# Two wider pitches in SBUF for the split operands of a three-layer fp32 kernel

## The reference, cut to what matters

```python
def peer_ffn(x, norm_ffn, w_query, sub_keys, expert_down, expert_up):
    xn = rmsnorm(x, norm_ffn)
    ...
        q = (xi @ w_query).reshape(B, PEER_CHUNK, PEER_HEADS, 2, PEER_HALF)
        s = jnp.einsum('bthpd,hpnd->bthpn', q, sub_keys)
        ... # top 16 of each half, top 16 of the pairs, idx, gates g
        u = jnp.take(expert_down, idx, axis=0)
        act = jax.nn.gelu(jnp.einsum('btd,bthkd->bthk', xi, u).astype(jnp.float32))
        v_sel = jnp.take(expert_up, idx, axis=0)
        return jnp.einsum('bthk,bthkd->btd', (g * act).astype(xi.dtype), v_sel)

x = x + hgrn_gmlp_mixer(x, ...);  x = x + peer_ffn(x, ...)   # layer 0
x = x + mla_moba_mixer(x, ...);   x = x + peer_ffn(x, ...)   # layer 1
x = x + merged(pool branch, dilated attention) @ w_out       # second block
return _rmsnorm(x, final_gain)
```

## Time and profile before

| | |
|---|---|
| median of 3 runs | 2086.08 us (2085.38 to 2088.28) |
| span of the profiled execution | 2086.7 us |
| PE busy | 2064.9 us (99%), 11,872 products |
| PE weight loads busy | 1768.4 us (85%) |
| DVE, ACT, POOL busy | 1462.7, 1290.6, 373.7 us |
| DMA | 376 MB, 180 GB/s |
| granted TensorE clock | 0.999 of full speed |

### The profile page before, as it was taken

How to read it: one execution, slowest core, us unless ns; L and a number is a source line. 1 busy time by engine, 2 the same in 40 slices (tenths; PEclk the granted TensorE clock), 3 DMA queues, 4 the chain that set the end, 5 groups by cost and what they waited for, 6 DMA issues and landing times.

```text
span 2086.7 us, 31212 instructions
## 1 busy us (share of the span) xinstructions
PE 2064.9 (99%) x11872; PEld 1768.4 (85%) x11872; DVE 1462.7 (70%) x2611; ACT 1290.6 (62%) x2205; POOL 373.7 (18%) x183
## 2 busy tenths in 40 slices
PE   8999999999999999999999999999999999999998
PEld 7788988888888888887888888888888888888888
DVE  7969988889855555567589888889655555543456
ACT  6665688877654444466656788777544444554674
POOL 1447700000000000012378000000000000045241
PEclk9999999999999999999999999999999999999999
DMA  6445755555565665664357555555566666676444
GB/s 228 152 162 170 227 180 166 169 172 166 172 194 190 196 193 191 195 214 141 122 171 222 182 164 171 163 172 171 187 195 192 192 194 191 205 221 195 129 153 140
DMA packets 108459, 376.25 MB, mean 180 GB/s; under 512 B 12373, under 2 KB 17909, under 8 KB 107413
## 3 DMA queue, kind: packets, MB, share of 16 engines
q1 hardware_dynamic: 107444, 369.00, 55.9%
q0 software_dynamic: 864, 5.24, 1.2%
HBM read 367.87 MB, written 1.08 MB: 177 GB/s over the span
## 4 chain that ended last, share of the span: by engine, by line
PE 91%; DVE 7%; ACT 1%; issue 0%; DMA 0%; POOL 0%; SPq 0%; DVEq 0%; ACTq 0%
PE ps L184 27%; PE ps L178 14%; PE ps L179 14%; PE ps L180 14%; PE ps L185 13%; PE ps L1086 3%; PE ps L1109 1%; PE ps L1065 1%; DVE WL L166 1%; DVE arena L1340 1%; DVE arena L791 1%; DVE arena L788 0%; DVE arena L1401 0%; DVE arena L1406 0%; DVE arena L1409 0%; DVE arena L1337 0%
## 5 line engine op out<-in xcount | busy, mean ns | idle before, releaser
L161 ACT ACTIVATE WH<-raw 128x1024 fp32r<-128x1024 f32 x680 | 717.2, 1057 | 451.3 <-PE ps L180 372.9
L184 PE MATMUL ps<-X,WH 128*128 128x512 f32 x2528 | 899.6, 400 | 0.1
L166 DVE TENSOR_TENSOR WL<-raw,WH 128x1024 fp32r<-128x1024 f32 x554 | 679.0, 1228 | 61.1 <-ACT WH L161 60.6
L185 PE MATMUL ps<-X,WL 128*128 128x256 f32 x2528 | 706.5, 279 | 0.0
L171 POOL TENSOR_TENSOR WL<-raw,WH 128x1024 fp32r<-128x1024 f32 x126 | 319.4, 2555 | 1597.2 <-ACT WH L161 1596.6
L184 PEld LDWEIGHTS ps<-X,WH 128*128 128x128 f32 x2528 | 474.5, 188 | 111.5 <-issue 1.8
L185 PEld LDWEIGHTS ps<-X,WL 128*128 128x128 f32 x2528 | 476.9, 189 | 0.1
L178 PE MATMUL ps<-WH,X 128*128 128x512 f32 (+1 forms) x960 | 378.3, 394 | 1.6 <-DVE X L390 0.9
L180 PE MATMUL ps<-WH,X 128*128 128x512 f32 (+1 forms) x960 | 373.9, 389 | 0.0
L179 PE MATMUL ps<-WL,X 128*128 128x512 f32 (+1 forms) x960 | 373.5, 389 | 0.0
L178 PEld LDWEIGHTS ps<-WH,X 128*128 128x128 f32 x960 | 180.6, 188 | 41.8 <-issue 2.1
(11 more groups left out here) (318 smaller groups left out, 2104.4 us busy)
## 6 DMA issues: line engine op xcount, KB each, us to landing
raw<-in_l_down_dram SPq DMA_DIRECT2D x256, 512.0 KB, 3.6
raw<-in_l_up_dram SPq DMA_DIRECT2D x256, 512.0 KB, 4.0
raw<-in_l_wq_dram SPq DMA_DIRECT2D x32, 512.0 KB, 3.5
raw<-in_w_qk_dram SPq DMA_DIRECT2D x24, 512.0 KB, 3.6
raw<-in_w_gates_dram SPq DMA_DIRECT2D x24, 512.0 KB, 3.5
raw<-in_l_nat_dram SPq DMA_DIRECT2D x16, 512.0 KB, 3.4
raw<-in_l_wout_dram SPq DMA_DIRECT2D x16, 512.0 KB, 3.5
raw<-in_l_win_dram SPq DMA_DIRECT2D x16, 512.0 KB, 4.1
```

Source lines behind the costliest of these rows:

```text
L161: a.activation(WH[:, i % NW, :], raw[:, i % NW, :], ACT.Copy).then_inc(w_high, 1)
L166: v.tensor_tensor(WL[:, i % NW, :], raw[:, i % NW, :], WH[:, i % NW, :], ALU.subtract).then_inc(w_low_v, 1)
L184: t.matmul(PS[:, bank, :], w[0], X2[:, k, :, :].rearrange("p w t -> p (w t)"), start=first, stop=False)
L185: return t.matmul(PS[:, bank, 0:256], w[1], X2[:, k, 0, :], start=False, stop=last)
```

## The change

The pitch from one slot of WH and of WL to the next grows from 4096 to 4112 bytes, and the pitch from one block of X2 to the next grows from 2048 to 2064 bytes. The views that the rest of the code uses keep their shapes.

```diff
@@ -17,6 +17,7 @@
 
 NW = 4
 SLOT = 1024
+SLOT_PITCH, X2_PITCH = SLOT + 4, 512 + 4
 NBIG = -1.0e30
 FILL = -3.0e38
 EPS = 1e-6
@@ -81,11 +82,11 @@
             return ctx.enter_context(nc.semaphore(name))
 
         X = sb("X", [128, 2, 1024])
-        X2 = sb("X2", [128, 8, 2, 256], F32R)
+        X2 = sb("X2", [128, 8, X2_PITCH], F32R)[:, :, 0:512].rearrange("p k (w t) -> p k w t", w=2)
         XH, XL = X2[:, :, 0, :], X2[:, :, 1, :]
         raw = sb("raw", [128, NW, SLOT])
-        WH = sb("WH", [128, NW, SLOT], F32R)
-        WL = sb("WL", [128, NW, SLOT], F32R)
+        WH = sb("WH", [128, NW, SLOT_PITCH], F32R)[:, :, 0:SLOT]
+        WL = sb("WL", [128, NW, SLOT_PITCH], F32R)[:, :, 0:SLOT]
         GP = sb("GP", [128, 2, 256], BF16)[:, :, :]
```

## The result

The changed kernel takes 2110.14 us, a median of 4 runs from 2108.42 to 2112.06, against 2085.73 us for the kernel before (2082.22 to 2088.28). The ratio is 1.0111, 95% interval [1.0096, 1.0126]. The change makes the kernel slower by 1.1%. The forecast was no change at 2086.0 us. The time lies inside the stated range, but its sign is that of rival B, which had a chance of 0.25.

The account below looks back on a forecast made before the run. PE's distances between matmul starts were taken to bound the kernel. Pairs, wide triples and narrow triples were each valued at 0, giving no change at 2086 us; their bounds ran from -116 to +50 us, the stated range from 2022 to 2118.

Parts of the forecast that it names:

- rival B: Up stage and pairs: even rhythm broken, +26 and +6 us, 2118 us (0.13); small form, pairs only, 2092 us (0.12).
- What bounds the kernel: Whole kernel: PE busy 99% of the span, so only the distances between starts of matmuls can move the time.
- The surplus in units of 16 columns: Steady PE distances: each product's surplus over its columns is close to a multiple of 16 columns, or 64 bytes.
- The relation of the operands: Distance modulo 64, always 0 before: steps with k in the pairs, changes only from chunk to chunk in the up stage.
- (2): Wide triples, 3888 products of 512 columns: between -43 and +23 us, taken as 0.
- Where in this range?: All PE products: load and moving operand meet at all distances within every load, so all three parts are near 0.
- (1): Pairs of 512 and 256 columns, 2528 of them: between -66 and +23 us, taken as 0.
- (3): Narrow triples, 624 products of 256 columns: between -7 and +4 us, taken as 0.
- A strong: All three kinds of product: only distance 0 costs, so -87 us, about 2007 us after VectorE's limit; chance 0.20.
- A mild: Pairs only: their slower rhythm is broken, -11 us, 2075 us; chance 0.15.
- C: Layout: the change doesn't do what it says; would show as the forecast does, no chance of its own.

Follow-up runs that it names:

- e17: Against the kernel before: slots of WH and WL 4112 bytes apart, padding keeping every start where it was modulo 256; 2100.7 us, 1.0071.
- e9: Against the kernel before: only the split rows in X2 moved by minus 16 bytes, up stage kept at distance 0; 2092.65 us, 1.0021.
- e13: Against the kernel before: X2, WH and WL start 16 bytes later modulo 256 while GH and GL stay; 2101.96 us, 1.0064.
- e15: Against the kernel before: only the split rows in X2 moved by plus 48 bytes, up stage kept at distance 0; 2084.27 us, 0.9985.
- e10: Against the kernel before: WH and WL start 256 bytes later as a whole, with their old pitch; 2089.56 us, 0.9995.
- e12: Against the kernel before: only the split rows in X2 moved by plus 16 bytes, up stage kept at distance 0; 2082.32 us, 0.9973.
- e14: Against the kernel before: only the split rows in X2 moved by plus 32 bytes, up stage kept at distance 0; 2083.35 us, 0.9973.
- e11: Against the kernel before: a pad of 64 bytes ahead of X2 moves all operands together; 2089.03 us, 1.0002.
- e1: Against the kernel before: only X2's blocks lie 2064 bytes apart, slots of WH and WL stay 4096 apart; 2109.84 us, 1.0106.

## Why the prediction was wrong

**What bounds the kernel** held: PE's starts set the time, no other engine's busy time changed by over 3 us, and the loss is in the distances between starts.

**The surplus in units of 16 columns** doesn't hold. The other layouts have steady means of 228.9 ns (64 bytes) and 231.7 ns (16 bytes), which are 549 and 556 columns and no multiple of 16. The pairs' 353 ns, read as 848 columns, is the mean of a cycle of 349, 350 and 361.

**The relation of the operands** changes more often than the prediction says. Under (2) it has one distance for a whole chunk. That is so modulo 64 for the chunks with GH and GL. In those with X2 the high and low parts of the rows lie in neighbouring blocks, 16 bytes apart modulo 64, and WL has moved by 64 bytes against WH. The kernel before has one relation throughout its up stages. The changed kernel has twelve kinds of chunk there (four slots, three places of the stationary tensor), and each has more than one relation. Changing isn't the main part of the loss, though: one constant relation of 32 bytes is slower still (1.0134), and e17 puts 0.9 of 5.4 ns on the changes.

**The step that failed is "Where in this range?"**, the claim that both streams pass all distances within every load, so that "another start changes the order of the meetings and not their number". The runs with one constant distance refute it: the same wide product takes 226.6, 231.6, 233.2, 233.2, 228.8 or 232.3 ns by nothing but where WH and WL start. The surplus over 213.3 ns of columns thus goes from 13.3 to 20 ns. An average over the meetings would have given one number for all of them. A larger modulus doesn't save the argument, because a slip of 64 bytes eight times in a load also passes all distances modulo 256. Two of its premises had no row: that what matters is how the two streams meet, and that an fp32r load takes the 107 ns of the plain fp32 products. In the same trace the f16 products of line 1086 follow each other at 57 ns, each with a load of 128 columns of its own.

**The terms.** (1) The pairs, valued at 0, cost 1.5 us in the trace, from bounds of -66 and +23. (2) The wide triples, valued at 0, cost 18.6 us, from bounds of -43 and +23. The upper bound, 233 ns from the value projection, held for every constant layout: it is the 233.3 of 32 and 48 bytes. The lower one never came near; in no run is the mean of the wide up products under 226.6 ns or that of the pairs under 347.6. (3) The narrow triples moved by under 1 us. The forecast took the middle of two bounds on the strength of an argument when the upper bound was a row of this very kind of product and the lower one came from plain fp32 products.

**The rivals.** B named the place, the price and the decision point rightly: the up stage over 228 ns, differing with the slot, +26 us for all wide products. The runs gave 232.0 ns and +18.6 us, since not every relation costs the full 6.7 ns, and the cost isn't a unit of 16 columns. Its second half, pairs from 347 to 353, didn't happen as a whole. A strong was wrong, as distance 0 is the best that was found for the up stage. Something of A mild is true, for the pairs alone: other relations do break their slow rhythm, and 0.27% are to be had from it. Under C I wrote that the later tensors move by multiples of 64 and that the change does what it says. That was right modulo 64 and beside the point, since 64 isn't the period: the tensors' growth had also moved WH by 128 and WL by 192 bytes against GH, and that is part of what was measured.

Two rules that the prediction names don't account for this. The Trainium skill ("TensorE: Matmul & The Clock Gate", "Step-by-step: what each phase is for") says that the next weights are loaded through a port of their own and take no bandwidth from the running product. Read as the prediction read it, that gives the same time for all layouts, and the start distances differ by 6.7 ns with the places of the two operands. So the reading fails for these fp32r products. Whether the load and the product clash in reading, or in something else that depends on both places, no run separates, since no kernel here multiplies without a load beside it. The Trainium skill's lines of 16 bytes ("SBUF — State Buffer", "SBUF: two separate sides") come with a condition that the prediction left out: two hits in a line are enough for full bandwidth. Four-byte numbers 8 bytes apart still have two, so the rule doesn't give the 233 ns of the earlier trace rows. It doesn't tell the layouts apart either, since all moves here are multiples of 16 bytes and leave the number of lines per operand as it was.

**What stays open** is the quantity itself. It repeats when one operand moves by 256 bytes and when all move by 64 (each tried once, from the layout of the kernel before), it isn't the distance alone (e9, e13) nor the moving operand's place alone (e15), and I have no model that gives the values of both tables. Why the pairs fall into different rhythms at one and the same layout wasn't settled either. It may also be why ten runs of e10 hold two at 2081.5 and 2082.6 us and eight from 2088.4 to 2091.6, but only one of them has a trace.

**A version that beats both.** The rows 16 or 32 bytes later with the up stage kept at distance 0 (e12, e14) take 0.9973 of the kernel before, [0.9964, 0.9982] and [0.9963, 0.9983], and so about 0.9973 / 1.0111 = 0.986 of the changed one. In e12's trace the pairs are 2528 x (347.7 - 351.1) = -8.6 us, and the wide products with the rows stationary give back 816 x 2.6 = 2.1 us. That is -6.5 us, near the -5.6 us of the ratio. The profiled execution shows PE's busy time 9.9 us lower than in the earlier trace rows:

```profile
PE 2055.0 (99%) x11872; PEld 1769.5 (85%) x11872; DVE 1459.8 (70%) x2611; ACT 1290.2 (62%) x2205; POOL 374.5 (18%) x183
```

## What to carry to other kernels

Where dense fp32r products set the time, the place of the stationary and the moving operand in SBUF is a parameter worth 1 to 3% of each product's time, and the profile shows it only as the distance between starts, at 0% idle and 99% busy. Give each kind of product one constant relation, but try a few shifts of whole tensors, since a constant one can also be a bad one (1.0134 with 32 bytes), and keep an eye on what a grown tensor does to all that are declared after it. A change of layout is to be tested for its period too, since a pad that is neutral by one modulus isn't by another.

## What the runs showed of the hardware that wasn't expected

- With one constant relation, a wide fp32r product (512 columns, a load of 128 beside it) starts 226.6 to 233.3 ns after the one before it in the mean, by the places of its operands alone; a pair of 512 and 256 columns takes 347.6 to 353.8 ns in the mean of a trace, and at one layout it can fall into more than one rhythm (e11).
- Moving one operand by 256 bytes changes nothing (226.6 and 226.6 ns), by 128 it does (232.3), by 64 it does (228.8).
- From distance 0, moving all operands by 64 bytes changes nothing (226.6); moving both of a product by 16 does (233.3 for 226.6).
- A disturbed rhythm needs up to ten products to come back: 224 to 236 ns one by one, and then 227 (e1).
